# A seven-product scheme on one more weight piece of each down projection, with one weight sum made in HBM

## The reference

```python
x = x + jnp.square(jax.nn.relu(h @ w_ff1[i])) @ w_ff2[i]          # first block: 4096 -> 1024
...
def swiglu(x, w_gate, w_up, w_down):                               # four times: 2816 -> 1024
    return (jax.nn.silu(x @ w_gate) * (x @ w_up)) @ w_down
x = x + FFN_RES_WEIGHT * swiglu(rms_norm(x, norm_ffn1[layer]), ...)
```

## Time and profile before

| | us |
|---|---|
| median of 3 runs (1414.39 to 1414.59) | 1414.42 |
| the profiled execution | 1414.2 |
| its span, first to last instruction | 1412.4 |
| TensorE busy | 1403.6 |
| VectorE busy | 1150.0 |
| ScalarE busy | 818.2 |
| GpSimd busy | 28.1 |

### The profile page before, as it was taken

The page is one execution under the profiler, slowest core; times in us unless marked ns, Lnnn a source line. Parts: engine busy times, 40 slices in busy tenths (PEclk is TensorE's granted clock), DMA queues, the critical chain, the costliest instruction groups (busy, mean ns, idle before and its releaser), DMA issues.

```text
span 1412.4 us, 22777 instructions
## 1 busy us (share of the span) xinstructions
PE 1403.6 (99%) x9163; PEld 1195.6 (85%) x9163; DVE 1150.0 (81%) x1601; ACT 818.2 (58%) x1110; POOL 28.1 (2%) x93
## 2 busy tenths in 40 slices
PE   8999999999999999999999999999999999999999
PEld 7988778888888888889878888888888887888887
DVE  6876686898878887988867888988889798688797
ACT  6735474565447655555866565555555557665562
POOL 1000000000001100000000000000000000000000
PEclk9999999999999999999999999999999999999999
DMA  9441236455565555455334455545555443355543
GB/s 346 174 150 63 91 120 208 173 185 201 197 220 179 202 186 184 174 209 191 141 119 177 179 196 192 208 178 188 201 179 198 164 177 147 113 201 194 181 177 119
DMA packets 37256, 250.15 MB, mean 177 GB/s; under 512 B 4256, under 2 KB 4384, under 8 KB 8096
## 3 DMA queue, kind: packets, MB, share of 16 engines
q1 hardware_dynamic: 36864, 248.51, 49.2%
q10 hardware_dynamic: 288, 0.19, 0.1%
HBM read 247.64 MB, written 1.05 MB: 176 GB/s over the span
## 4 chain that ended last, share of the span: by engine, by line
PE 98%; DVE 1%; DMA 0%; ACT 0%; issue 0%; SPq 0%; DVEq 0%; ACTq 0%
PE ps L2254 24%; PE ps L2173 16%; PE ps L2175 15%; PE ps L2174 15%; PE ps L2261 13%; PE ps L2426 2%; PE ps L2238 1%; PE ps L2242 1%; PE ps L2244 1%; PE ps L2338 1%; PE ps L2639 1%; PE ps L2619 1%; PE ps L2628 1%; PE ps L2411 0%; PE ps L2563 0%; DMA a<-xtin 0%
## 5 line engine op out<-in xcount | busy, mean ns | idle before, releaser
L3061 DVE TENSOR_TENSOR lo<-raw,hi 128x2048 fp32r<-128x2048 f32 (+1 forms) x230 | 522.4, 2271 | 63.7 <-ACT hi L2682 60.9
L2682 ACT CAST hi<-raw 128x2048 fp32r<-128x2048 f32 (+1 forms) x230 | 436.5, 1899 | 192.6 <-PE ps L2175 123.2
L2254 PE MATMUL ps<-h,hi 128*128 128x512 f32 x1504 | 359.0, 390 | 0.0
L2254 PEld LDWEIGHTS ps<-h,hi 128*128 128x128 f32 x1504 | 276.4, 188 | 52.4
L2173 PE MATMUL ps<-hi,a 128*128 128x512 f32 x516 | 204.6, 397 | 0.0
L2175 PE MATMUL ps<-hi,a 128*128 128x512 f32 x516 | 201.4, 390 | 0.0
L2174 PE MATMUL ps<-lo,a 128*128 128x512 f32 x516 | 201.1, 390 | 0.0
L2261 PEld LDWEIGHTS ps<-h,lo 128*128 128x128 f32 x1504 | 192.2, 190 | 7.8
L2261 PE MATMUL ps<-h,lo 128*128 128x256 f32 x1504 | 194.4, 282 | 0.0
L2886 ACT COPY a<-ps 128x256 f32<-128x256 f32 x208 | 76.3, 372 | 157.1 <-PE ps L2254 84.8
L3029 DVE TENSOR_TENSOR a<-ps,a 128x256 f32<-128x256 f32 x208 | 82.2, 419 | 41.7 <-ACT a L2886 41.6
(11 more groups left out here) (379 smaller groups left out, 1827.8 us busy)
## 6 DMA issues: line engine op xcount, KB each, us to landing
raw<-ws SPq DMA_DIRECT2D x227, 1024.0 KB, 4.8
raw<-ws SPq DMA_DIRECT2D x4, 512.0 KB, 8.0
X<-xin SPq DMA_DIRECT2D x8, 256.0 KB, 7.0
raw<-ws SPq DMA_DIRECT2D x4, 256.0 KB, 5.8
out<-X SPq DMA_DIRECT2D x4, 256.0 KB, 2.1
small<-small SPq DMA_DIRECT2D x1, 992.5 KB, 7.4
const<-const SPq DMA_DIRECT2D x1, 900.0 KB, 7.9
a<-xtin SPq DMA_DIRECT2D x3, 256.0 KB, 5.8
```

What stands on the lines that cost most here:

```text
L2254: t = e.matmul(b2(s["slots"][u]), wh[:, k, 128 * u:128 * u + 128], h2[:, k, :, :], start=k == 0, stop=last)
L2682: e.copy(hi[j % NSPL][:, n], raw[j % NRAW][:, n]).then_inc(hi_ready, 1)
L3061: e.tensor_tensor(lo[j % NSPL][:, n], raw[j % NRAW][:, n], hi[j % NSPL][:, n].bitcast(F), ALU.subtract).then_inc(lo_ready, 1)
```

## The change

`SEVENS` gets a sixth piece in each of the five down projections: pieces 1, 3, 4, 5, 6, 7 of the gated downs (before: without 5), and 3, 5, 6, 8, 9, 11 of `w_ff2` (before: 3, 5, 7, 9, 11). The gated downs have three sets of sums and `w_ff2` two. The sum of the first two weight blocks of each of the 30 seven pieces is no longer made on the chip: at the start, after the 15th piece is split, GpSimd issues 30 DMAs that copy block 1 of such a piece to a new HBM tensor `block_sums`, and 30 DMAs that add block 0 to it there. SP then loads a seven piece with three DMAs (block 0, the sum, blocks 2 and 3) in place of one, after a wait for the group of six sums that it belongs to. "w_sums" has three operations in place of four, "hi" no longer waits for it, and signs in `mix`, "w_sums" and `seven_add` change with the scheme; `mix` and `seven_add` keep their numbers of operations. "w_sums" of a gated down is no longer put ahead of the piece before.

```diff
-SEVENS = {"a": (1, 3, 4, 6, 7), "s": (3, 5, 7, 9, 11)}
+SEVENS = {"a": (1, 3, 4, 5, 6, 7), "s": (3, 5, 6, 8, 9, 11)}
...
-        by_src = {"a": Sevens(5, (aH, aL), [Arena(14 * 4096), Arena(h_at - arena0)], Arena(17 * 4096), (sgm[0], sgm[1], sgs[0])),
-                  "s": Sevens(5, (sH, sL), [Arena(h_at - arena0)], late_ar, (rl[0], rl[1], h_rest))}
+        by_src = {"a": Sevens(6, (aH, aL), [set_at(14 * 4096), set_at(11 * 4096), set_at(h_at - arena0)], Arena(17 * 4096),
+                              (sgm[0], sgm[1], sgs[0])),
+                  "s": Sevens(6, (sH, sL), [set_at(h_at - arena0), set_at(0, 8 * 4096)], late_ar, (rl[0], rl[1], h_rest))}
...
         def emit_lo(j):
-            if not weaving[0] and j + 1 in sevens and sevens[j + 1][0] == "a" and sevens[j + 1][1]:
-                sums_early(j + 1)
...
-            emit("hi", act=1.9, j=j, after=freed.get(j - NSPL), sums=summed[j][0] if j in sevens else None)
+            emit("hi", act=1.9, j=j, after=freed.get(j - NSPL))
...
-                    e.tensor_tensor(WS[:, 1, :], w[:, 3, :], w[:, 1, :], ALU.subtract)
-                    e.tensor_tensor(w[:, 1, :], w[:, 1, :], w[:, 0, :], ALU.subtract).then_inc(wsum_v.sem, 1)
-                    e.wait_ge(wsum_v.sem, s["own"][0])
-                    e.tensor_tensor(WS[:, 0, :], w[:, 3, :], w[:, 1, :], ALU.subtract).then_inc(wsum_v.sem, 1)
-                    e.wait_ge(wsum_v.sem, s["own"][1])
-                    e.tensor_tensor(WS[:, 2, :], w[:, 2, :], WS[:, 0, :], ALU.subtract).then_inc(wsum_v.sem, 1)
+                    t = e.tensor_tensor(WS[:, 0, :], w[:, 3, :], w[:, 1, :], ALU.add)
+                    t.then_inc(wsum_v.sem, 1)
+                    e.wait_ge(wsum_v.sem, s["own"][-2])
+                    e.tensor_tensor(WS[:, 1, :], WS[:, 0, :], w[:, 0, :], ALU.subtract)
+                    e.tensor_tensor(WS[:, 2, :], w[:, 2, :], WS[:, 0, :], ALU.add).then_inc(wsum_v.sem, 1)
...
+                    if s["v"] == 1:
+                        e.wait_ge(lo_ready, 15)
+                        for g in range(5):
+                            for n in range(per_stage * g, per_stage * g + per_stage):
+                                e.dma_start(block_sums[n], ws[made_sums[n]][:, 512:1024]).then_inc(copied_out[g], 16)
+                        for g in range(5):
+                            e.wait_ge(copied_out[g], 16 * per_stage)
+                            for n in range(per_stage * g, per_stage * g + per_stage):
+                                e.dma_start(block_sums[n], ws[made_sums[n]][:, 0:512], accum_op=ALU.add).then_inc(sums_out[g], 16)
...
-                    e.dma_start(raw[i][:, :], ws[j + NRAW]).then_inc(raw_in[i], 16)
+                    if made(j + NRAW):
+                        n = made_sums.index(j + NRAW)
+                        e.wait_ge(sums_out[n // per_stage], 16 * per_stage)
+                        e.dma_start(raw[i][:, 0:512], ws[j + NRAW][:, 0:512]).then_inc(raw_in[i], 16)
+                        e.dma_start(raw[i][:, 512:1024], block_sums[n]).then_inc(raw_in[i], 16)
+                        e.dma_start(raw[i][:, 1024:2048], ws[j + NRAW][:, 1024:2048]).then_inc(raw_in[i], 16)
+                    else:
+                        e.dma_start(raw[i][:, :], ws[j + NRAW]).then_inc(raw_in[i], 16)
```

More of the change, by code:

```diff
@@ L238, in program @@
         x_in = [[sem(f"x_in{b}{h}") for h in range(2)] for b in range(2)]
+        copied_out = [sem(f"block_copied{g}") for g in range(5)]
+        sums_out = [sem(f"block_sums_out{g}") for g in range(5)]
         raw_in = [sem(f"raw_in{i}") for i in range(NRAW)]
@@ L498, in __init__ @@
                 self.H, self.L = acts
-                self.sums = [(ar_([128, 3, 512], R), ar_([128, 3, 512], R), ar_.again([128, 3, 512])) for ar_ in sums]
+                self.sums = [(low([128, 3, 512], R), high([128, 3, 512], R), low.again([128, 3, 512])) for low, high in sums]
                 self.ML = [mixed([128, 3, 128], R) for _ in range(n)]
@@ L503, in __init__, with set_at @@
                 self.parts = [t[:, :, :].rearrange("p a n -> p (a n)") for t in parts]
-        by_src = {"a": Sevens(5, (aH, aL), [Arena(14 * 4096), Arena(h_at - arena0)], Arena(17 * 4096), (sgm[0], sgm[1], sgs[0])),
-                  "s": Sevens(5, (sH, sL), [Arena(h_at - arena0)], late_ar, (rl[0], rl[1], h_rest))}
+        def set_at(at_, high_at=None):
+            low = Arena(at_)
+            return low, low if high_at is None else Arena(high_at)
+        by_src = {"a": Sevens(6, (aH, aL), [set_at(14 * 4096), set_at(11 * 4096), set_at(h_at - arena0)], Arena(17 * 4096),
+                              (sgm[0], sgm[1], sgs[0])),
+                  "s": Sevens(6, (sH, sL), [set_at(h_at - arena0), set_at(0, 8 * 4096)], late_ar, (rl[0], rl[1], h_rest))}
         def sums_of(j):
@@ L511, in sums_of, with made, landed @@
             return by_src[src].sums[unit % len(by_src[src].sums)]
+        def made(j):
+            return j in sevens
+        def landed(j):
+            return 16 * sum(3 if made(n) else 1 for n in range(j % NRAW, j + 1, NRAW))
         sevens = {}
@@ L517, in program @@
                 sevens[i] = (src, SEVENS[src].index(n // 2))
+        made_sums = sorted(sevens)
+        per_stage = len(SEVENS["a"])
+        assert len(SEVENS["s"]) == per_stage
+        block_sums = nc.dram_tensor("block_sums", (len(made_sums), 128, 512), F, kind="Internal").ap()
         ta = Arena(0)
@@ L622, in sums_early @@
                 sets = len(by_src[src].sums)
-                in_h = unit == sets - 1
-                summed[j] = [wsum_v.add() for _ in range(3)]
+                first = j - SEVENS[src][unit]
+                if (src, unit) in (("a", 2), ("s", 0)):
+                    over = freed[first - 1]
+                elif (src, unit) == ("a", 1):
+                    over = (ff_v.sem, ff_v.n)
+                else:
+                    over = freed[first + 2] if (src, unit) == ("s", 1) else None
+                summed[j] = [wsum_v.add() for _ in range(2)]
                 emit("w_sums", dve=2.6, j=j, own=summed[j], used=sum(n < j for n in sevens) - min(unit, sets - 1),
-                     after=freed[j - SEVENS[src][unit] - 1] if in_h else None)
+                     after=over)
         def split_hi():
@@ L2675, in scalar_program @@
                     j = s["j"]
-                    e.wait_ge(raw_in[j % NRAW], 16 * (j // NRAW + 1))
+                    e.wait_ge(raw_in[j % NRAW], landed(j))
                     if s["after"]:
                         e.wait_ge(s["after"][0], s["after"][1])
-                    if s["sums"]:
-                        e.wait_ge(wsum_v.sem, s["sums"])
                     n = slice(LAST_AT[j] if j < 3 else 0, PIECE)
@@ L3040, in mix @@
                     e.tensor_tensor(z[:, 1, :], a[:, 0, first], a[:, 0, second], ALU.subtract)
-                    e.tensor_tensor(a[:, 0, second], a[:, 0, second], a[:, 1, second], ALU.add).then_inc(mix_v.sem, 1)
+                    e.tensor_tensor(a[:, 0, second], a[:, 0, second], a[:, 1, second], ALU.subtract).then_inc(mix_v.sem, 1)
                     e.wait_ge(mix_v.sem, v[0])
@@ L3044, in mix @@
                     e.wait_ge(mix_v.sem, v[1])
-                    e.tensor_tensor(z[:, 2, :], a[:, 1, first], z[:, 0, :], ALU.subtract).then_inc(mix_v.sem, 1)
+                    e.tensor_tensor(z[:, 2, :], a[:, 1, first], z[:, 0, :], ALU.add).then_inc(mix_v.sem, 1)
             def mix_lo(mix_):
@@ L3073, in vector_program @@
                     w = raw[s["j"] % NRAW][:, :].rearrange("p (q n) -> p q n", q=4)
-                    e.wait_ge(raw_in[s["j"] % NRAW], 16 * (s["j"] // NRAW + 1))
+                    e.wait_ge(raw_in[s["j"] % NRAW], landed(s["j"]))
                     if s["used"]:
@@ L3103, in vector_program @@
                     ready(five)
-                    t = e.scalar_tensor_tensor(to[0, 1], banks[five.b][:, :], f[0], to[0, 1], ALU.mult, ALU.add)
-                    t.then_inc(seven_v.sem, 1)
+                    e.wait_ge(seven_v.sem, v[0])
+                    e.tensor_tensor(copy, banks[five.b][:, :], u, ALU.subtract).then_inc(seven_v.sem, 1)
                     ready(seven)
-                    e.wait_ge(seven_v.sem, v[0])
                     e.tensor_tensor(w, banks[seven.b][:, :], u, ALU.add).then_inc(seven_v.sem, 1)
-                    t = e.scalar_tensor_tensor(to[1, 1], banks[five.b][:, :], f[1], to[1, 1], ALU.mult, ALU.add)
-                    t.then_inc(seven_v.sem, 1)
                     e.wait_ge(seven_v.sem, v[1])
-                    t = e.scalar_tensor_tensor(to[0, 1], u, f[0], to[0, 1], ALU.mult, ALU.add)
+                    t = e.scalar_tensor_tensor(to[0, 1], copy, f[0], to[0, 1], ALU.mult, ALU.add)
                     t.then_inc(seven_v.sem, 1)
                     e.wait_ge(seven_v.sem, v[2])
+                    e.tensor_tensor(u, banks[five.b][:, :], w, ALU.subtract).then_inc(seven_v.sem, 1)
```

(4 more changed lines are left out.)

## The result

The changed kernel is slower. Its median is 1425.14 us (1424.49 to 1425.86, 4 runs), beside 1414.41 for the kernel before on the same chip (1414.38 to 1414.59, 4 runs): ratio 1.0074, 95% interval 1.0061 to 1.0086. The forecast was 1411.0. The profiled execution took 1425.75 us with a span of 1423.9, 11.5 more than before.

The account below looks back on a forecast made before the run. TensorE, busy for 99% of the span, was taken as the bound. Fifteen matmuls fewer gave 3.40 us, all other terms nothing: 1414.42 - 3.40 = 1411.0, forecast 1410.2 to 1411.6 (0.66), wider range 1410.2 to 1415.0.

Parts of the forecast that it names:

- The matmuls removed: Five down projections: one piece each goes from 24 matmuls to 21, 0.68 us per down, 3.40 us gained in all.
- VectorE in the gated downs: Run of five seven pieces: VectorE's last "w_lo" still ends 1.2 us ahead of its product on TensorE; cost nothing.
- VectorE becomes the bound: Rival, run of five in gated downs: 0.4 us more per seven piece gives 1414.2, 0.6 gives 1418; chance 0.09.
- `w_ff1`, `w_ff2`, `seven_add`, SP and the loads: VectorE's work there, SP's extra issues and the piece loads all stay covered: nothing for each.
- The 60 HBM DMAs: GpSimd's copies and adds from 97.1 us: about 1 us per issue, ending between about 145 and 225; cost nothing.
- Friction in the weave: Rival placed in the weave, its details cut from the text; chance 0.14, of which 0.10 no change.
- GpSimd late: Rival: norm's roots at 253.30 wait behind 60 issues if above 2.6 us each; at 2.8, 1422 or so; chance 0.11.
- The last line of what would show it wrong: Wrong if TensorE idles before L2173 in a down, before L2353 near 256, or anywhere between 97 and 253.

Follow-up runs that it names:

- the spread version: Changed kernel with each projection's 6 copies and 6 adds issued after a norm's roots ahead of large matmuls, not all 60 in the weave: 1411.03 us, ratio 0.9976.

## Why the prediction was wrong

**The matmuls removed: right.** The working gave 0.68 us per down and 3.40 in all; the five stretches lost 0.63 to 0.75, 3.5 in all, and the spread version measures 1414.50 - 1411.03 = 3.47.

**VectorE in the gated downs: right.** The last "w_lo" was to end 1.2 us ahead of its product. Sums, "lo" and "w_lo" of the last seven pieces of the run, and the product, in the changed kernel:

```profile
618.45 0.68 DVE L3102 TENSOR_TENSOR a<-raw 128x512 f32<-128x512 f32 x1
619.17 0.69 DVE L3105 TENSOR_TENSOR a<-a,raw 128x512 f32<-128x512 f32 x1
619.78 0.68 DVE L3106 TENSOR_TENSOR a<-raw,a 128x512 f32<-128x512 f32 x1
620.38 2.28 DVE L3083 TENSOR_TENSOR lo<-raw,hi 128x2048 fp32r<-128x2048 f32 x1
622.58 1.75 DVE L3110 TENSOR_TENSOR a<-a,a 128x1536 fp32r<-128x1536 f32 x1
...
625.37 0.39 PE L2197 MATMUL ps<-a,a 128*128 128x512 f32 x1
```

622.58 + 1.75 = 624.33, 1.04 us ahead. The three sums take 1.93 us, as forecast (1.94). The version with the fourth operation shows the other side of that margin: 0.8 us more per piece, and it was gone. By the formula of the rival "VectorE becomes the bound" that is 5 x 0.8 - 1.2 = 2.8 us per gated down, and 3.97 were measured; there "hi" waits for a sum as well. So the wall lies between nothing and 0.8 us more per piece, as the rival says. Where between was not measured.

**`w_ff1`, `w_ff2`, `seven_add`, SP and the loads: right,** nothing each. A whole-piece load still lands in 4.8 us. In the burst it took 8.6, and stayed hidden.

**"The 60 HBM DMAs. ... Both ends are in time, so the cost is nothing": this is the step that failed.** Its bounds held. Issue took 0.52 and 0.84 us where "about 1" was taken, the DMAs ended near 176 inside "between about 145 and 225", and GpSimd was free 129 us before its next work. But the step asked only two questions, whether the queue's owner is in time and whether the piece loads stay hidden. It left out a third user of the same 16 DMA engines, the loads of TensorE's instructions, and it priced competition by the share of bytes (2 x 7.86 MB against one piece every 9 us) where the wait at the full engines counts. It cost 15.0 us, shown by adding the DMAs alone to the kernel before, which cost 14.3. That the starved thing is the instruction supply is shown by the stops themselves, at multiples of 256 instructions from the first and each 1.2 to 1.6 us behind the end of an instruction load, and by their absence where few instructions are used or the engines are not full.

**The rivals.** "Friction in the weave" named the right stretch, at 0.14 and mostly as no change. No run shows a size for the friction that the range up to 1415.0 takes in; what the runs showed of that stretch is 15.0 us lost with the 60 DMAs, 8.4 with the copies alone and nothing with the copies one by one. "GpSimd late" had a time of 1422, near the measured one, for a reason that did not occur. Its waits for copies cost GpSimd 0.97 us. The last line of what would show it wrong, "TensorE shows idle ... anywhere between 97 and 253", is the one that did.

**How GpSimd's DMAs ran.** In a row the copies were issued 0.52 us apart and the adds 0.84, under the 2.6 us per issue at which "GpSimd late" puts its wall; the copies landed a median of 10.7 us after their issue in the kernel with the copies alone. One at a time they started 3.8 to 6.6 us apart, HBM to HBM. Nor did a busy VectorE hold up the issues: in the kernel with all DMAs behind the weave, GpSimd issued the 30 copies in 15.78 us, 0.53 us each, with VectorE busy for 13.29 of 15.70 us of that, mostly in operations with two inputs (TENSOR_TENSOR); others were not tried. The instruction loads of 16 KB stand in the kernel before as well, ten from 97 to 153, and there they cost nothing: TensorE has no "issue" idle in the weave. With the DMA engines full (a share of 0.94 to 1.11 up to 153) it has 10.7 us of it.

**What stays open.** Whether an instruction load waits at the DMA engines, behind the bulk packets, or for HBM, is not told apart; TensorE's stops among the adds, at 205 GB/s, as well as among the copies, at some 320, speak for the engines, but no transfer that leaves HBM out was tried. That q8 serves TensorE is inferred, from its count and from the stops. What part of the 1.2 to 1.6 us between the end of a load and TensorE's next instruction is owed to the full engines is open too, as no stop without them is on record.

## What to carry to other kernels

An engine's own instructions are a stream of loads too. Here it was 73 loads of 16 KB for TensorE, by their count and its stops. Where TensorE runs many small matmuls (52 matmuls and weight loads per us here, 16 KB of instructions every 4.8 us), count that stream as a user of the DMA engines, and don't queue bulk DMAs over it. Put them where the engines run few large instructions (1411.03 us so), or keep one in flight at a time (TensorE busy for 103.00 of 103.00 us). With full engines an instruction load came every 6.3 to 8.2 us in the changed kernel; a stretch that used one every 7.6 us lost nothing, and one that needed one every 4.8 to 5.8 us lost 15.0 us, clock included. When a change is slower with every engine still 99% busy, compare marks along the time axis and look for "issue" in the timeline: here a gain of 3.5 us and a loss of 15.0 stood 100 us apart.

## What the runs showed that was not expected

- A 16 KB instruction load was about 1 us long with the DMA engines free (0.88 to 1.45 us from 97 to 153 before) or full (0.93 to 1.10 after). With full engines the next one came late: 6.3 to 8.2 us apart in the changed kernel, in place of down to 4.
- A load of 16 KB held 256 instructions of TensorE: the stops lie a multiple of 256 instructions apart, in the changed kernel and in those with the DMAs or the copies alone (two of them, after 2241 and 3009, in all four).
- TensorE stopped in the middle of a run of equal 64x64 matmuls, for up to 3.66 us, and in that idle the granted clock went from 1.00 to 0.50 for some 7 us. The length of the idle alone did not decide: with the copies alone from GpSimd the clock fell after idles of 2.66 and 1.67 us, and in the changed kernel and with the copies from SP it stayed at 1.00 after idles of up to 2.32 and 2.06.
- Copies of 256 KB from HBM to HBM ran at some 320 GB/s together, and DMAs that add at some 205, both with the engines full and by the profile's count of bytes. GpSimd issues the first in 0.52 us and the second in 0.84.
- Thirty such copies cost TensorE 8.4 us when queued together and nothing (253.39 against 253.30) when issued one by one over 136 us.
